# Turning one head's probabilities with VectorE through a DRAM exchange, in the second head group of a hybrid attention block

## What is computed

```python
def mixer_b(q, k, v, rel_table):        # 8 heads of 64, chunks of 64 tokens
    qc = q.reshape(b, nc, CHUNK, B_HEADS, HEAD_DIM)
    kb = band_gather(k..., B_BAND)      # own chunk and 8 before it
    vb = band_gather(v..., B_BAND)
    logits = einsum('bcqhd,bckhd->bhcqk', qc, kb) * SCALE
    logits = logits + bias              # by relative distance, one row per head
    logits = where(valid, logits, NEG)
    p = softmax(logits, axis=-1)
    out = einsum('bhcqk,bckhd->bcqhd', p, vb)
```

## Time and profile before

| | |
|---|---|
| median of three runs | 1033.53 us (1033.47 to 1033.95) |
| span of the profiled execution | 1031.9 us, first to last instruction |
| TensorE busy | 1023.0 us, 99% of the span |
| VectorE, ScalarE busy | 770.9 us and 470.5 us |
| steps 32 to 53 | about 171.2 to 290.0 us |
| granted TensorE clock | 0.999 of full speed |

### The profile page before, as it was taken

How to read it: one execution, slowest core, us unless ns; L and a number is a source line. 1 busy time by engine, 2 the same in 40 slices (tenths; PEclk the granted TensorE clock), 3 DMA queues, 4 the chain that set the end, 5 groups by cost and what they waited for, 6 DMA issues and landing times.

```text
span 1031.9 us, 15795 instructions
## 1 busy us (share of the span) xinstructions
PE 1023.0 (99%) x5525; PEld 851.0 (82%) x5525; DVE 770.9 (75%) x1506; ACT 470.5 (46%) x978; POOL 219.7 (21%) x218
## 2 busy tenths in 40 slices
PE   9999999999999999999999999999999999999997
PEld 8899887788778888878888888888888888888886
DVE  4955677867688578888988788786444777778997
ACT  6632355545477567836221221311344445454562
POOL 5200000000000003148675674761100000000000
PEclk9999999999999999999999999999999999999999
DMA  9835442111071474045444434446777733454344
GB/s 202 222 98 136 108 134 77 42 47 37 11 225 43 123 188 159 21 143 212 171 167 155 163 134 152 163 144 225 243 243 242 229 103 92 143 194 142 93 142 164
DMA packets 135071, 147.92 MB, mean 143 GB/s; under 512 B 72248, under 2 KB 85440, under 8 KB 132944
## 3 DMA queue, kind: packets, MB, share of 16 engines
q1 hardware_dynamic: 133920, 146.68, 45.7%
q10 hardware_dynamic: 688, 0.20, 0.1%
q0 software_dynamic: 384, 0.04, 0.0%
HBM read 103.65 MB, written 47.49 MB: 146 GB/s over the span
## 4 chain that ended last, share of the span: by engine, by line
PE 94%; DVE 3%; issue 1%; DMA 1%; ACT 0%; POOL 0%; DVEq 0%; ACTq 0%; POOLq 0%
PE ps L2242 27%; PE ps L2244 27%; PE ps L2243 27%; PE ps L2451 3%; PE ps L2465 3%; PE ps L2432 2%; PE ps L2376 1%; DVE wc_lo L1918 1%; PE ps L2411 1%; PE ps L2584 1%; PE ps L2586 1%; PE ps L2572 1%; DMA up_raw<-in_w_up 1%; DVE b_lo L1907 1%; PE ps L2254 0%
## 5 line engine op out<-in xcount | busy, mean ns | idle before, releaser
L2242 PE MATMUL ps<-b_hi,wc_hi 128*128 128x512 f32 x448 | 174.6, 390 | 0.5 <-DVE wc_lo L1918 0.5
L2243 PE MATMUL ps<-tm_lo,sm_hi 128*128 128x512 f32 (+1 forms) x450 | 174.6, 388 | 0.0
L2244 PE MATMUL ps<-tm_hi,sm_lo 128*128 128x512 f32 (+1 forms) x450 | 174.6, 388 | 0.0
L2242 PE MATMUL ps<-tm_hi,sm_hi 128*128 128x512 f32 (+1 forms) x450 | 174.6, 388 | 0.0
L2244 PE MATMUL ps<-b_hi,wc_lo 128*128 128x512 f32 x448 | 174.3, 389 | 0.0
L2243 PE MATMUL ps<-b_lo,wc_hi 128*128 128x512 f32 x448 | 174.3, 389 | 0.0
L1485 ACT ACTIVATE sm_hi<-sm_raw 128x512 fp32r<-128x512 f32 x112 | 70.7, 631 | 161.8 <-DMA sm_raw<-u_matrices 161.8
L2146 DVE TENSOR_TENSOR sm_lo<-sm_raw,sm_hi 128x512 fp32r<-128x512 f32 x112 | 77.4, 691 | 77.9 <-ACT sm_hi L1485 77.3
L2242 PEld LDWEIGHTS ps<-b_hi,wc_hi 128*128 128x128 f32 x448 | 84.1, 188 | 18.3 <-DVE wc_lo L1918 0.9
L2242 PEld LDWEIGHTS ps<-tm_hi,sm_hi 128*128 128x128 f32 x450 | 84.5, 188 | 17.6
L2244 PEld LDWEIGHTS ps<-tm_hi,sm_lo 128*128 128x128 f32 x450 | 84.5, 188 | 17.4
(11 more groups left out here) (261 smaller groups left out, 2063.2 us busy)
## 6 DMA issues: line engine op xcount, KB each, us to landing
u_matrices<-stage SPq DMA_DIRECT2D x112, 256.0 KB, 2.0
sm_raw<-u_matrices SPq DMA_DIRECT2D x112, 256.0 KB, 2.6
up_raw<-in_w_up SPq DMA_DIRECT2D x16, 1024.0 KB, 5.0
w<-in_w_down SPq DMA_DIRECT2D x64, 256.0 KB, 3.8
w_raw<-in_w_in SPq DMA_DIRECT2D x8, 512.0 KB, 3.5
xr<-in_x SPq DMA_DIRECT2D x8, 512.0 KB, 4.3
x_rows<-xr SPq DMA_DIRECT2D x8, 512.0 KB, 4.1
xf<-x_rows SPq DMA_DIRECT2D x8, 512.0 KB, 3.5
```

Source lines behind the costliest of these rows:

```text
L2242: pe.matmul(out, w_hi_, x_hi_, start=start, stop=False)
L2243: pe.matmul(out, w_hi_, x_lo_, start=False, stop=False)
L2244: return pe.matmul(out, w_lo_, x_hi_, start=False, stop=stop)
```

## The change

For steps 32 to 53 (`turned_b(n)`), head 0's probabilities no longer go through TensorE. Head 1's do as before.

- ScalarE's `normalize(n)` multiplies head 0's probabilities by the reciprocal (VectorE keeps the reciprocal, drops the multiplication) and writes them in another order of columns into one buffer (`prob_b` slot 2). Head 0's scores of all these steps share slot 0.
- SyncE's `exchange_step(n)` waits for it, stores it to DRAM with one DMA of 128 x 4 pieces, waits until that has landed and until VectorE has turned step n - 1, and loads it back with one DMA of 128 rows into `turn_in`.
- VectorE's `turn_probs(n)` turns the 32x32 blocks of `turn_in` into `probT_b`, in step n + 1, behind that step's `normalize` and, in the even paired steps, ahead of the scores of step n + 2.
- TensorE's `weigh(n)` reads head 0's turned tiles in pieces of 32 columns and writes them to PSUM columns four apart.
- The chunks become one of head 1's tiles (copied by ScalarE), in five-tile steps 4 and 1 (the 1 copied by VectorE).
- `load_bias` and `load_fill` are put between the exchanges of SyncE's queue.

```diff
-    if paired(n) and nk <= 2:
-        return [(0, 2 * nk, nk == 1)]
+    if turned_b(n):
+        return [(nk, nk, True)] if nk < B_KEYS else [(nk, 4, True), (nk + 4, 1, False)]
...
+            def exchange_step(n):
+                m = keys_of(n) * 32
+                sp.wait_ge(s_pb, pb0 + n - A_STEPS + 1)
+                tile = pb_dram[n - A_STEPS, 0:512 * m]
+                sp.dma_start(tile.rearrange("(a p m) -> p a m", a=4, m=m),
+                             sent_probs(n).rearrange("p (a m) -> p a m", m=m)).then_inc(s_pst, 16)
+                sp.wait_ge(s_pst, pst0 + 16 * (n - A_STEPS + 1))
+                if n == A_STEPS:
+                    sp.wait_ge(s_pv, A_STEPS)
+                else:
+                    sp.wait_ge(s_tb, tb0 + n - A_STEPS)
+                sp.dma_start(turn_in[:, 0:4 * m], tile.rearrange("(p m) -> p m", p=P)).then_inc(s_pld, 16)
...
+            for n in range(A_STEPS, LATE):
+                exchange_step(n)
+                if n == A_STEPS:
+                    load_bias(5)
+                elif n % T == T - 1:
+                    sp.wait_ge(s_nm, 2 * n + 2)
+                    load_bias(n // T + 2)
+                elif n % 4 == 1 and n // 4 - 2 < FILL_TILES:
+                    load_fill(n // 4 - 2)
...
+            def normalize(n):                       # ScalarE
+                at = 2 * (n % 2)
+                act.wait_ge(s_ri, 2 * n + 1)
+                if n > A_STEPS:
+                    act.wait_ge(s_pst, pst0 + 16 * (n - A_STEPS))
+                nc.scalar.activation(quarters_first(sent_probs(n)), blocks_first(prob_of(n, 0)[:, first_column(n):]),
+                                     ACT.Copy, scale=rinv[0][:, at:at + 1]).then_inc(s_pb, 1)
...
+            def turn_probs(n):                      # VectorE
+                dve.wait_ge(s_pld, pld0 + 16 * (n - A_STEPS + 1))
+                dve.wait_ge(s_pv, n - 1)
+                cols = slice(0, keys_of(n) * P)
+                nc.vector.transpose(prob_t(n, 0)[:, cols], turn_in[:, cols]).then_inc(s_tb, 1)
...
                 take(done)
-                if n < STEPS and not (paired(n) and n % 2):
+                if n < STEPS and not odd:
                     scores(n)
...
-                if n >= LATE or n == A_STEPS + 2:
+                if n > LATE:
                     copies_of(n - 1)
-                if paired(n) and n % T == 2:
-                    scores(n + 1)
-                if n < STEPS and not (paired(n) and n % 2):
+                if n < STEPS and not odd:
                     for hh in range(2):
                         normalize(n, hh)
-                if n < LATE and n != A_STEPS + 2 and not paired(n - 1):
+                if A_STEPS < n <= LATE:
+                    turn_probs(n - 1)
+                if paired(n) and not odd:
+                    scores(n + 1)
+                if n <= LATE:
                     copies_of(n - 1)
...
+                if turned_b(n):                     # TensorE, weigh(n)
+                    pe.wait_ge(s_tb, tb0 + n - A_STEPS + 1)
...
+                        if hh == 0 and turned_b(n):
+                            out_ = out_.rearrange("p (j c) -> p c j", c=4)
```

More of the change, by code:

```diff
@@ L485, in turn, with prob_slot, sent_probs, probs_made @@
             return r % 2 if T <= r < 2 * T else 0
+        def prob_slot(n, hh):
+            return 0 if hh == 0 and turned_b(n) else 2 * (n % 2) + hh
         def prob_of(n, hh):
-            return prob_b[:, 2 * (n % 2) + hh]
+            return prob_b[:, prob_slot(n, hh)]
+        def sent_probs(n):
+            return prob_b[:, 2, 0:keys_of(n) * P]
+        def probs_made(n, hh):
+            return 2 * A_STEPS + (n - A_STEPS + 1 if turned_b(n) else LATE - A_STEPS + 2 * (n - LATE) + hh + 1)
         def prob_t(n, hh):
@@ L500, in chunk_copy @@
             out = ps[:, CHUNK_BANKS[n, c][0], 0:count * P]
-            if nk == B_KEYS:
+            if nk == B_KEYS and not turned_b(n):
                 return heads.rearrange("p h n -> p (h n)")[:, first * P:(first + count) * P], out
-            nh = count // nk
-            return heads[:, first // nk:first // nk + nh, 0:nk * P], out.rearrange("p (h n) -> p h n", h=nh)
+            return heads[:, first // nk, first % nk * P:(first % nk + count) * P], out
         def odd_values(t):
@@ L1247, in _ @@
             for n in range(A_STEPS, STEPS + 3):
+                odd = paired(n) and n % 2 == 1
                 if n == A_STEPS + 2:
@@ L1251, in _ @@
                     store_mix((n - 6) // 4)
-                if A_STEPS < n < LATE and not paired(n - 1):
+                if odd:
+                    normalize(n)
+                if A_STEPS < n <= LATE and not paired(n - 1):
                     copy_chunk(n - 1, 0)
@@ L1255, in _ @@
                     tiles_hi(halves_done(n - 1))
-                if n < STEPS and not (paired(n) and n % 2):
-                    for m in (n, n + 1) if paired(n) else (n,):
+                if n < STEPS and not odd:
+                    for hh in range(2):
+                        exp(n, hh)
+                    if turned_b(n):
+                        normalize(n)
+                    if paired(n):
                         for hh in range(2):
-                            exp(m, hh)
+                            exp(n + 1, hh)
                 if n == A_STEPS:
@@ L1262, in _ @@
                     store_first_mix(n)
-                if paired(n) and n % 2:
+                if odd:
                     for m in (n - 1, n):
[L1265 to L1268, removed]
+                        copy_chunk(m, 0)
+                if LATE < n <= STEPS:
+                    for c in range(len(chunks_of(n - 1))):
                         if chunks_of(n - 1)[c][2]:
                             copy_chunk(n - 1, c)
-                    if n != LATE:
-                        tiles_hi(halves_done(n - 1))
+                if n <= STEPS and n != LATE:
+                    tiles_hi(halves_done(n - 1))
                 splits(n)
@@ L2447, in transposes @@
                     pe.wait_ge(s_pta if chunks_of(former[0])[former[1]][2] else s_ptd, copied(*former))
-                pe.wait_ge(s_p, 2 * n + (start + count - 1) // nk + 1)
+                pe.wait_ge(s_p, probs_made(n, (start + count - 1) // nk))
                 for i in range(count):
@@ L2513, in _ @@
                 if paired(n) and n % 2:
-                    for c in range(len(chunks_of(n - 1))):
-                        transposes(n - 1, c)
+                    transposes(n - 1, 0)
                     if n % T == 1:
@@ L2518, in _ @@
                 elif not paired(n - 1):
-                    transposes(n - 1, 0)
-                    transposes(n - 1, 1)
+                    for c in range(len(chunks_of(n - 1))):
+                        transposes(n - 1, c)
                 for m in range(first, end):
```

84 lines of the change are left out of this document (45 added, 39 removed).

## The result

The changed kernel took 1040.81 us (median of 4 runs, 1039.43 to 1047.11) against 1033.57 for the kernel before, measured beside it (4 runs, 1033.47 to 1033.95): 1.0082 times as long, 95% interval 1.0054 to 1.0110. It is slower, by 7.2 us, where no measurable change was forecast, and it lies 1.1 us above the range.

What follows compares the result with a forecast made beforehand. TensorE, busy 99% of the span, was taken to bound the kernel. Span 1031.9 us less 8.6 saved plus 8.3 of waits gives 1031.6; with 1.6 to the median, 1033.2 us, range 1028.3 to 1039.7.

Steps and rivals of the forecast that it cites:

- The saving: TensorE, steps 32 to 53: 80 head 0 transposes spared at 0.107 us each, 8.6 us; five-tile step 5.10 to 4.56.
- VectorE and ScalarE as busy time: Steps 32 to 53: both engines' added work stays far below the window, so it is costed at nothing.
- the order of columns in head 0's products: TensorE's 160 head 0 records with strided PSUM writes: taken as nothing; upper end, half speed, +8.5 us.
- the sum of the waits: TensorE's waits for head 0's turned probabilities: 0.8 + 2.5 + 2.3 + 0.95 + 1.7 = 8.3 us.
- rival A: The forecast itself: saving and waits cancel, 1033.2 us, own range 1030.5 to 1035.7; chance 0.45.
- 35 at 37, 43 at 45, 51 at 53: Weighing four-tile steps: VectorE's turn stands behind the five-tile step's normalisation; wait 0.77 us each, 2.3 in all.
- 37 at 39 and 45 at 47: Weighing at the step's start: TensorE comes at 10.29, turned probabilities ready at 10.65; wait 0.4 us each, 0.8 in all.
- 39 at 41 and 47 at 49: Weighing: VectorE's scores stand between turn and copy, ready at 11.35, TensorE at 10.09; wait 1.26 us each, 2.5 in all.
- 33 at 35: Weighing 33 at step 35: turn at 186.0, TensorE at 185.2; 0.8 plus 0.15 for step 35's probabilities, 0.95 us.
- weights for the fills ... are covered too; if not, a 3 us load would be late once: SyncE's queue: fill weights, issued three steps ahead of their split, cost nothing; otherwise one 3 us load is late.
- The way out: 53 weighed at 55, no fills from step 54: 1.07 us of spared transposes lost plus 0.65 more, 1.7 us.
- Rival D: Slower: the exchange takes 6 us, 1.2 more at 35, 39, 41, 47, 49 and 55, +7.2, 1040.4 us; chance 0.08.

Runs made afterwards that it cites:

- dense version: Changed kernel with head 0's products written to PSUM in consecutive columns, output order not the reference's: 1039.56 us, 1.0063 times before.
- The last experiment: Kernel with both order edits, step 53 back and weighing ahead of the first fill; there `load_fill` moved to n % 4 == 2: 1032.44 us, 0.9987.
- the version with the weighing between transposes and fills: Changed kernel with VectorE's new order, step 53 back on TensorE, and odd steps' weighing of n - 2 behind transposes, ahead of fills: 1032.18 us, 0.9987.
- the later weighing: Changed kernel with the odd steps' weighing of n - 2 moved behind scores, transposes and first two fills; alone 1038.05 us, 1.0048.

## Why the prediction was wrong

**The saving was right.** 240 transposes became 160, and a five-tile step takes 4.52 (197.94 to 202.46 between starts) where 4.56 was forecast. The small difference comes from a sentence that was wrong: not every group of transposes is still there. A five-tile step had eight and two with fills between them; now its five stand together, and the fills are broken up once less. With the table above, 8.6 us saved against 14.9 lost gives the 6.0 of the profiled execution. The median lies 1.1 above that execution, and the longer executions are those with the lower mean clock.

**VectorE and ScalarE as busy time** cost nothing, as said, and so did the order of columns in head 0's products. The Trainium skill ("PSUM — Partial Sum Buffer", Specifications) says that any non-contiguous access slows matmuls significantly; for these writes, four fp32 columns apart, the measurement decides otherwise: 273 ns with and without. The reason that the forecast gave for taking nothing, that a record is as long as a weight load and a stream of 128 columns, rests on no row; the dense version is what shows it.

**The step that failed is the sum of the waits, 8.3 us, which measured 14.9.** The mechanism, rival A's, was right in kind: every forecast wait stands where it was put, none at 43 and 51. What was mis-sized is above all the exchange within it: from the store's issue to the turn's start it took 5.45, 5.15 and 5.40 us at 37, 39 and 45, 6.69 at 47 and 5.80 at 53, where 4.85 was summed for each. And two kinds of wait were put at nothing: the fills for VectorE's evacuation, and the transposes of 54 for their bank. By term:

- *35 at 37, 43 at 45, 51 at 53:* 0.77 forecast, 0.78 to 0.80 measured. These hang on VectorE's order alone, and removing the exchange left them.
- *37 at 39 and 45 at 47,* "0.4 each": 1.1. The undisturbed store takes 2.48 (2.2 was taken, from a store of 256 KB), the load some 2.95 to the turn's start and not 2.65 (205.16 to 208.12 at step 37), some 0.1 more goes at the store's issue, and about 0.25 are the fills waiting for `tmp`, whose evacuation stands behind the turn on VectorE.
- *39 at 41 and 47 at 49,* "1.26 each": 1.70 and 3.24. The first is 1.27 of weighing and 0.42 of fills. In the second the store took 3.94 instead of 2.48. This second one is the largest single miss. The five-tile chain was summed as if each transfer had the queues to itself. Without the exchange both fall to 0.35: they hang on the transfer, and VectorE's order alone makes no wait there.
- *33 at 35,* 0.95: 1.4. VectorE turned 33 at 186.01, to 0.01 where it was put; idle time of 0.28 and 0.37 is seen at the weighing and at the transposes of 35, and what the rest is was not told apart.
- *"weights for the fills ... are covered too; if not, a 3 us load would be late once":* the other way round. The 512 KB weight load itself was on time, but the store issued 1 us behind it (185.25) took 3.6 against 2.2 for the same size undisturbed. In the two profiles of the changed kernel that cost little; in that of the dense version, whose order is the same, the store took 4.29 and the fills of step 36 waited 1.69. With the orders changed it is a wait of 1 us there, since the turn of 34, the evacuation and the fill stand in a row behind it. The last experiment shows that it is the load: moved, it hits the next store instead, and so at 38, 43, 46 and 47.
- *The way out,* 1.7: 3.6. The load of step 53 took 3.3 to land with the output weights' loads (L881) right behind it, and the transposes of 54 waited 1.69 for a PSUM bank whose copy stood behind that turn. This wait was not in the list. About 1.0 of the 3.6 is the clock (twenty records in 2.26 instead of 1.24), and 1.8 are there without any exchange.

Rival D came nearest in time (1040.4), by its mechanism only in part: it moved all of these waits by 1.2, while the exchange was longer by 0.3 to 0.6 where undisturbed, by 0.95 at 53 and by 1.8 at 47. That its time is so near is in part luck, since fills, bank and clock, which it does not have, make up what it counts too much. It had a chance of 0.08, and the stated range ended below its own time.

**How much hangs on the exchange** is shown by leaving it out: 9.5 us. How much the places in the two orders cost is shown by moving both: 7.4 us, which brings the kernel back to the time before. The two are not parts of one sum, since the better orders win mostly by giving the exchange more time. **Why the best versions win only about 1.5 us of 8** is read from the profile of the version with the weighing between transposes and fills: idle time of 0.45 at step 35, 0.97 at 36 and 0.20 at 41, and then a loss with no idle time at all. From the scores of step 42 to those of step 50 it takes 42.30 (224.76 to 267.06), before 43.79; with 30 transposes spared it would be 40.58. So 1.7 go in eight steps, in which each odd step has one more group of weighings and one more break of TensorE's work. Over all of steps 32 to 53 the same sum gives 6.2, of which 1.6 is idle time that the timeline shows; the other 4.5 show none. A part of it can be seen: five transposes take 0.69 to the next start where a weighing follows (209.14 to 209.83) and 0.52 where a fill does (203.35 to 203.87). That such switches are the whole 1.7 is argued, not shown.

**What stays open.** Step 47's store took 2.85 to 4.61 in the five profiles in which TensorE weighs at the old place (VectorE's order moved or not), 2.47 or 2.48 in the four with the later weighing, and 3.41 in the last, behind a load of weights. In the slow five the trace shows an instruction fetch in a queue of its own (q14) about 2.2 us behind the store's issue. In the changed kernel the transfer ends in a tail of 6 to 26 GB/s, where it moved about 300 before, and fifteen of the store's sixteen completions are there after 2.84 us and the last after 3.92. The store of step 44 has such a fetch 2.0 us behind its issue in all ten profiles, and took 3.18 to 3.23 in each; no store of 2.48 has one. That the fetch delays the store is an inference, not tried. And why the clock falls behind an idle stretch in some executions and not in others is open: the repetition of the changed kernel had an idle stretch of 3.03 us at step 49, the changed kernel one of 2.68 and the dense version one of 1.69, all with the clock at 1.00.

## What to carry to other kernels

A chain that is nearly as long as its cover must be summed with its transfers among the others that are issued next to it, and each event that an in-order engine does behind the wait (here evacuations and bank copies) counted as a wait of its own. When two engines in order meet at a rendezvous, moving one's place alone passes the wait on; move both. A version without the transfer, even where its result is not the reference's, tells in one run how much the whole exchange can give back.

## What the runs showed of the hardware that was not expected

- A store of 320 KB in 512 pieces to DRAM took 2.46 to 2.54 us from issue to the load's issue at six of the ten five-tile steps, in every run that has them; a load back in 128 rows took 2.7 in the median (1.8 to 3.3, all sizes; in the changed kernel). Behind a 512 KB load issued 1 us earlier, a 192 KB store took 3.4 to 4.3 in place of 2.2; behind one issued 2 us earlier, 320 KB took 4.1 to 5.1 at step 38 and 2.7 to 3.0 at step 46, and 2.49 and 2.47 once that load was issued elsewhere.
- TensorE's granted clock fell from 2.4 to 1.2 GHz (0.50) near the end of an idle stretch of 3.37 us, with step 53 back on TensorE, and about 0.9 us behind one of 1.69 us on the changed kernel's way out, each costing about 1 us at the next weighing alone. It did not fall at others of 1.69 to 3.03 us. The kernel before repeated within 0.5 us in its four executions beside the changed one (1032.94 to 1036.23 in the 58 beside the experiments, one of 4505.8 left out); the changed one spread by 8, and by 4 in the repetition.
